# A chunked delta rule on one core: value products in the crossed quarters of TensorE, and a new order of one turn

## The reference, cut to what matters

```python
def step(S, inp):
    r_t, w_t, k_t, v_t, kk_t, b_t = inp
    sa = jnp.einsum('bhvk,bhk->bhv', S, kk_t)
    S = S * w_t[:, :, None, :] - sa[..., None] * b_t[:, :, None, :] + v_t[..., None] * k_t[:, :, None, :]
    return S, jnp.einsum('bhvk,bhk->bhv', S, r_t)

S_fin, ys = lax.scan(step, wkv0.astype(f32), seq)
y = jnp.moveaxis(ys, 0, 1)
m = jnp.mean(y, -1, keepdims=True)
var = jnp.mean(jnp.square(y - m), -1, keepdims=True)
y = (y - m) * lax.rsqrt(var + GN_EPS) * gn_g + gn_b
y = y + jnp.sum(rh * kh * r_k, -1, keepdims=True) * vh
out = (y * jax.nn.silu(g)) @ w_out
```

## Time and profile before

| what | value |
|---|---|
| runs | 1472.65, 1472.77 and 1475.62 us, median 1472.77 |
| span of the profiled execution | 1471.6 us, first to last instruction |
| delta rule in it | from about 491 to 861 us |
| PE busy over the whole span | 1411.4 us (96%), its weight loads 1281.0 us (87%) |
| DVE, ACT, POOL busy over the whole span | 794.4, 575.6, 249.8 us (54%, 39%, 17%) |

### The profile page before, as it was taken

The page is one execution under the profiler, slowest core; times in us unless marked ns, Lnnn a source line. Parts: engine busy times, 40 slices in busy tenths (PEclk is TensorE's granted clock), DMA queues, the critical chain, the costliest instruction groups (busy, mean ns, idle before and its releaser), DMA issues. The chain is left out here.

```text
span 1471.6 us, 37545 instructions
## 1 busy us (share of the span) xinstructions
PE 1411.4 (96%) x16154; PEld 1281.0 (87%) x16154; DVE 794.4 (54%) x1588; ACT 575.6 (39%) x1178; POOL 249.8 (17%) x351
## 2 busy tenths in 40 slices
PE   7999999999999899999999979999999999998997
PEld 7989899887899899999999858899999997665885
DVE  6737345777831377777777753651112122775545
ACT  6726246777832022222122232441111132886324
POOL 0000000000000256555554700000001000214000
PEclk9999999999999999999999999999999998999999
DMA  5723222567596244335534255024234236431202
GB/s 207 225 60 89 74 89 90 143 188 233 167 256 179 75 97 100 74 87 118 118 88 105 68 196 186 29 111 130 88 90 119 73 108 184 137 105 33 88 29 94
DMA packets 246358, 174.00 MB, mean 118 GB/s; under 512 B 150799, under 2 KB 220367, under 8 KB 245279
## 3 DMA queue, kind: packets, MB, share of 16 engines
q1 hardware_dynamic: 214231, 156.64, 36.9%
q10 hardware_dynamic: 31968, 15.04, 3.6%
HBM read 111.49 MB, written 60.46 MB: 117 GB/s over the span
## 5 line engine op out<-in xcount | busy, mean ns | idle before, releaser
L369 PE MATMUL mix_acc<-mix_high,mix_w_high 128*128 128x364 f32 (+1 forms) x768 | 178.2, 341 | 11.2 <-ACT mix_high L435 9.9
L369 PE MATMUL mix_acc<-mix_low,mix_w_high 128*128 128x364 f32 (+1 forms) x768 | 172.1, 333 | 0.6 <-DVE mix_low L589 0.6
L369 PE MATMUL mix_acc<-mix_high,mix_w_low 128*128 128x364 f32 (+1 forms) x768 | 171.1, 331 | 0.0
L369 PEld LDWEIGHTS mix_acc<-mix_high,mix_w_high 128*128 128x128 f32 x768 | 130.4, 190 | 30.1 <-issue 28.3
L369 PEld LDWEIGHTS mix_acc<-mix_low,mix_w_high 128*128 128x128 f32 x768 | 133.4, 190 | 1.2 <-DVE mix_low L589 0.9
L369 PEld LDWEIGHTS mix_acc<-mix_high,mix_w_low 128*128 128x128 f32 x768 | 133.9, 190 | 0.0
L1528 PE MATMUL out_acc<-qkvg_room_r_high,qkvg_room_w_high 128*128 128x364 f32 (+1 forms) x320 | 105.8, 331 | 2.2 <-DVE qkvg_room_w_low L1880 2.2
L603 DVE TENSOR_TENSOR mix_w_low<-mix_wt,mix_w_high 128x1024 fp32r<-128x1024 f32 x32 | 39.2, 1224 | 126.1 <-ACT mix_w_high L441 125.8
L1528 PE MATMUL out_acc<-qkvg_room_r_low,qkvg_room_w_high 128*128 128x364 f32 (+1 forms) x320 | 105.1, 329 | 0.0
L1528 PE MATMUL out_acc<-qkvg_room_r_high,qkvg_room_w_low 128*128 128x364 f32 (+1 forms) x320 | 105.1, 329 | 0.0
L1878 DVE CAST qkvg_room_w_high<-qkvg_room_wt 128x1024 fp32r<-128x1024 f32 x20 | 14.0, 699 | 156.9 <-DMA qkvg_room_wt<-in_w_att 156.9
(11 more groups left out here) (280 smaller groups left out, 3412.6 us busy)
## 6 DMA issues: line engine op xcount, KB each, us to landing
mix_wt<-in_w_in SPq DMA_DIRECT2D x32, 512.0 KB, 4.6
qkvg_room_wt<-in_w_att SPq DMA_DIRECT2D x20, 512.0 KB, 3.8
delta_bk<-scr_bk SPq DMA_DIRECT2D x17, 512.0 KB, 4.7
delta_kr<-scr_kr SPq DMA_DIRECT2D x17, 512.0 KB, 7.2
scr_kr<-mix_outs SPq DMA_DIRECT2D x16, 512.0 KB, 3.9
scr_bk<-mix_outs SPq DMA_DIRECT2D x16, 512.0 KB, 4.6
early_xpad<-in_xpad SPq DMA_DIRECT2D x8, 548.5 KB, 8.5
scr_xg<-early_xs SPq DMA_DIRECT2D x8, 544.0 KB, 3.0
```

What stands on the lines that cost most here:

```text
L369: mm = pe.matmul(acc[:, s, k, 0:width], w[:, s, d, :], r[:, d, n0:n0 + width], start=d == 0 and q == 0, stop=d == DT - 1 and q == 2)
```

## The change

It has two parts.

**The crossed quarters.** The products with k (k = 1) write to the other half: `make_grams` and `turn_rows` send operands of half `p` to half `f` of `FLIPPED`. Blocks 2 and 3 of `grams` and `rows[:, :, 1]` then lie on the opposite half from their head. v is loaded with its halves swapped (two DMAs of 64 partitions in place of one of 128), so that the products with v read half `f` and write half `p`. The bonus, which needs v as it was, reads a further copy, `v_plain`, loaded by a further DMA. Each value product (`value_product`) is taken out of its accumulation group and now stands beside a product in the diagonal quarters: u beside block 3·v, block 1·u beside rows1·v, the third `make_lm` beside block 2·v. The other half of each sum (`end_z`, `end_y`, `end_s`) follows in a loop of its own. Bank `gram0` now takes the products with b and `gram1` those with k, four pairs each, so that grams of a chunk come in two portions instead of four; DVE masks each portion with two instructions of the same size as before.

**The order.** u, y and the state's products of the chunk behind come first in a turn, before the inverse's first level. `turn_y` and `spread_blocks` move from the head of a turn to its end, one chunk earlier. On DVE the gating moves likewise, and the solve is cut in two, columns 0 to 3 at the end of a turn and 4 to 6 at the head of the next. POOL makes two level masks instead of three (the third level reads `grams` itself), and `end_state` and `small` change places with other steps.

```diff
+def other_half(half):
+    return slice(64 - half.start, 128 - half.start)
-        sp.dma_start(d["v_rows"][:, 0], scr["vt"][0]).then_inc(d["v_loaded"][0], 16)
+        for half in (slice(0, 64), slice(64, 128)):
+            sp.dma_start(d["v_rows"][half, 0], scr["vt"][0, other_half(half)]).then_inc(d["v_loaded"][0], 16)
...
+                    for p, f in zip(HALVES, FLIPPED):
+                        sp.dma_start(v_rows[f, c % 3], scr["vt"][c, p]).then_inc(v_loaded[c % 3], 16)
+
+                def load_plain_values(c):
+                    if c >= 3:
                         sp.wait_ge(bonus_made, 2 * (c - 2))
-                    sp.dma_start(v_rows[:, c % 3], scr["vt"][c]).then_inc(v_loaded[c % 3], 16)
+                    sp.dma_start(v_plain[:, c % 3], scr["vt"][c]).then_inc(plain_loaded[c % 3], 16)
...
+                    for j in range(4):
+                        pair = 4 * h + j
+                        for p in HALVES:
+                            first = pe.matmul(gram_bank[0][p, 128 * j:128 * j + 128], bk[p, c % 2, 0, pair, :], kr[p, c % 4, :, pair, :], start=True, stop=True)
+                        for p, f in zip(HALVES, FLIPPED):
+                            second = pe.matmul(gram_bank[1][f, 128 * j:128 * j + 128], bk[p, c % 2, 1, pair, :], kr[p, c % 4, :, pair, :], start=True, stop=True)
...
+                def value_product(c, pair, bank, stands, begun):
+                    for p, f in zip(HALVES, FLIPPED):
+                        mm = pe.matmul(bank[p, 64 * pair:64 * pair + 64], stands[f], v_rows[f, c % 3, pair, :], start=pair == 0, stop=False, skip_group_check=True)
+                    if pair == DT - 1:
+                        mm.then_inc(begun, 1)
...
                 for i in TURNS:
                     front, behind = i + 1, i - 1
-                    if 0 <= i - 2 < SAMPLE - 1:
-                        turn_y(i - 2)
-                    if live(i):
-                        spread_blocks(i)
                     if live(behind):
                         make_u(behind)
...
+                    if live(behind):
+                        rest_of_y(behind)
+                        end_y(behind)
                     if 0 <= behind < SAMPLE:
-                        make_s(behind)
-                    if live(behind):
-                        make_y(behind)
...
+                        end_s(behind)
                     if 0 <= i < SAMPLE:
                         make_lm(i, 0)
...
                     if 0 <= i < SAMPLE:
+                        wait_for_z(i)
+                        make_lm(i, 2, lambda pair: begin_z(i, pair))
                         grow(i, 2)
+                        end_z(i)
...
+                    if 0 <= behind < SAMPLE:
+                        turn_y(behind)
+                    if live(front):
+                        spread_blocks(front)
```

336 lines of the change are left out of this document (175 added, 161 removed).

## The result

The changed kernel takes 1482.18 us (median of 20 runs, 1474.3 to 1488.6) against 1472.71 for the kernel before: a ratio of 1.0056, with a 95% interval from 1.0044 to 1.0069. It is slower by half a per cent, where 1424 us was predicted with a range of 1410 to 1458. Its profiled execution has a span of 1480.4 us, 8.8 more than before.

What follows compares the result with a forecast made beforehand. PE's products were taken as the bound; fifteen turns cut from 20.57 to 17.55 us save 45.3, the first turn 4, the tail 0. Together 49 off a 1471.6 span, plus 1.2 to the median, gave 1424 us (range 1410 to 1458).

Steps and rivals of the forecast that it cites:

- What bounds the kernel now: Steady delta-rule turns: PE's products set the time, 19.8 us, or 20.3 with pauses, of 20.57 a turn.
- What the crossed quarters are worth: PE's blocks: crossed products run beside diagonal ones, saving 5.5 us of 19.8 a turn, leaving about 14.3.
- (a): Crossed pairs sharing rows load weights one after the other, so only grams halve; 28 us saved, 1445 us; chance 0.18.
- (b): The array takes only two records at once; 1470 us, shown by starts of u above 20 us apart; chance 0.09.
- What is late next: A steady turn: DVE's chain and PE's blocks both end at 17.05 us, with 2.4 us of waiting in PE.
- The pauses at issue stay: PE in each turn: the number of records is unchanged, so 0.5 us of pauses is kept.
- forecast of 17.55: Length of a steady turn in us: 17.05 from the walk plus 0.5 of pauses, against 20.57 before.
- Rival (e): Four quarters use up instructions faster, so pauses grow one us a turn; 1439 us, counted within the forecast's 0.62.
- Rival (c): PE's clock falls to 1.2 GHz, making turns about 30 us; with six such turns 1497 us; chance 0.05.
- The first turn: Start of the stage, up to u of chunk 0: doubled blocks and grams save 4 us.
- The edits costed at nothing: v's split load and plain copy, added semaphores, split solve and moved gate were all to cost no time.
- POOL's cover of 0.4 us: In a turn POOL's decay and gain end at about 15.1 us, against DVE's need at 15.5.

Runs made afterwards that it cites:

- m3: The changed kernel with all products back in the diagonal quarters, so two quarters run at a time; 1476.5 us, 1.0021 of the kernel before.
- p1: As p0, but the crossed products of the values and k's rows stand in blocks of their own behind the diagonal ones; 1468.6 us, ratio 0.9955.
- p0: The changed kernel, but for chunk 0 the grams with b stand ahead of those with k; 1475.9 us, 1.0027 of the kernel before.
- m4: The changed kernel without the value products of six of eight head pairs, 144 PE instructions fewer a turn, outputs wrong; 1449.5 us, ratio 0.9829.
- p2: As p1, with rows made by transposes, 96 PE instructions fewer a turn, and a later wait for the new state; 1461.7 us, ratio 0.9917.
- the streams' kernel: A separate kernel, computing nothing of the reference, with streams of independent products on PE alone; 256 instructions took 3.5 to 4.3 us without loads.
- r1: The kernel before with a forced PE pause of about 2.2 us in each of 17 turns, by three ACT copies; 1526.0 us, ratio 1.0362.

## Why the prediction was wrong, point by point

- **What bounds the kernel now: PE's products.** Right: with light loads the kernel before has turns of 19.82 us without a gap. But a second limit stood right under it, 4.6 pieces of instructions at some 4 us, and the prediction did not look for it, though the pauses at issue were in its rows. With its own loads the kernel before stood at that second limit as well.
- **What the crossed quarters are worth.** Right in size for the array: 0.96, 0.93 and 0.95 us for the blocks that were taken at 0.95 and 0.9. Rivals (a) and (b) are out by these rows, although the starts of u, 20.4 us apart, are what the prediction named as the sign of (b): a sign in the turn's length alone can't tell the array from what feeds it.
- **What is late next: DVE at 17.05 us.** Never reached. PE's waits for DVE and ACT were 0.2 us a turn instead of 2.4.
- **"The pauses at issue stay: the number of records is the same."** This is the step that failed. Not their number alone but how fast they are used up sets the pauses: 256 instructions in 2.1 us instead of 4. They went from 0.5 to 3.5 us a turn, the largest term of what was lost against the forecast of 17.55. Rival (e) named the mechanism and priced it at 1 us a turn, without a row that bore on it. The rows that would have: the earlier trace rows has 32 records and as many loads in 0.98 us, so 256 instructions in 3.9; the packets of the instruction queue could have been set against that.
- **Rival (c), the clock.** It was looked for as a state of the whole stage. It comes as a toll: 1.6 us behind most pauses of 2 us (forced pauses), and a mean of 0.95 in the steady part. PE was busy 231.66 / 13.97 = 16.6 us a turn instead of 14.3; the clock is a cause of these 2.3 us. An estimate of its share: a mean of 0.95 between 0.5 and 1.00 is a tenth of the time at 1.2 GHz, where half of the work is lost, so 1.0 us a turn at most. The other 1.3 us are not explained by any run. 16.6 + 3.5 + 0.2 = 20.3.
- **The first turn: 4 us saved.** Lost 9.8, of which 8.5 in the stage. The new portions made PE wait for DVE's masks of both banks, as m3 shows with products that are not shortened, and the clock fell between the waits. The change to two portions was not costed, and only the waits of later turns had been walked, not those of the first.
- **The edits costed at nothing.** The semaphores and SP's queue cost nothing that shows: PE's list of waits has no load in it. The transfers do, but not where the prediction looked: light loads gain 28.6 us in the changed kernel and 11 before. What of this is the added copy of v was not separated.
- **POOL's cover of 0.4 us.** Not put to the test, since the turns never came near 17.05 us; DVE's wait for the gain is one of 1.2 us in the whole stage.

## What to carry to other kernels

Before making an engine's instructions shorter, count how many of them run in a microsecond: PE got no more than 256 in 3.5 to 4.8 us here, so a block that uses them up in 2 us only moves the time into pauses at issue, and most pauses of 2 us brought half clock for a while behind them. Where a kernel is near that limit, the even pace (p1 against p0) and fewer instructions (m4, and p2 with a single-pass transpose for two products of two passes) were worth more than more quarters at once. When a step is cut into new portions, ask which bank each must find free. A pause at "issue" in a profile can be a resource with a limit: set the gaps between pauses against 256 instructions before calling it noise.

## What the runs showed of the hardware

- PE's instructions come in pieces of 256: in the streams' kernel, with four quarters of 64 columns, 3.5 to 4.3 us each alone and 4.3 to 4.8 beside loads at 180 to 210 GB/s; in the changed kernel three pieces took 4.4 to 5.4.
- All four quarters of 64 x 64 run at once, also two that share their rows: in the streams' kernel 256 instructions at full clock in 2.1 us, against 4.0 for two quarters.
- A forced pause of 2.0 us in each turn sent the clock to 1.2 GHz from about 1 us behind it, for some 3 us, in twelve turns of fifteen (r1).
- Products of 16 columns in two quarters, without any pause, ran at full clock for 3.5 us and then at 0.51 for 20 us, though the records had PE busy throughout; with 64 columns in two quarters and 128 in four it stayed at 1.00.
